# Rotary tables behind the first reciprocal, and finer first transfers, in a one-core encoder block with a product-key expert layer

## The chip, the cores and the metric

The kernel runs on one core of one Trainium2 chip. The metric is the device time of one execution in microseconds (us). TensorE is called PE here, VectorE DVE, ScalarE ACT, GpSimd POOL, and SyncE, which only issues transfers, SP.

## The reference

One layer over 256 tokens of width 1024, batch 1, all in float32:

```python
n = rmsnorm(h, norm_mix)
qa, ka, va, qb, kb, vb, ga, gb = split(n @ w_in)        # 1024 -> 5120 columns
y_a = differential_attention(qa, ka, va, lam, ...)      # 4 heads, partial rotary on q and k
y_b = neighbourhood_attention(qb, kb, vb, na_rpb)       # 8 heads, windows of a grid, bias
merged = sigmoid(ga) * (y_a @ w_proj_a) + sigmoid(gb) * (y_b @ w_proj_b)
h = h + merged @ w_out
h = h + peer_ffn(rmsnorm(h, norm_ffn), w_query, sub_keys, expert_u, expert_v)
out = rmsnorm(h, norm_final)
```

The rotary part turns the first 16 of each head's 64 dimensions: `rot = concat(x1*c - x2*s, x2*c + x1*s)`, with cosine and sine tables over the positions. The expert layer picks 16 of 16,384 single-neuron experts for each of 8 heads and each token; the kernel computes all experts densely for 240 tokens and gathers rows for the other 16.

## The kernel before

**Tiles.** Every weight matrix is cut into tiles of 1024 x 128, and one stream of them (512 KB each) runs through the whole kernel: tile numbers 0 to 7 are q and k of the differential attention (`T_QA`, `T_KA`), 8 to 11 its v (`T_VA`), 12 to 27 the other attention and the first gates, up to the projections, `w_out` and the queries; then come 128 tiles of the experts' input side (u) and 128 of their output side (v). A tile has 8 chunks (`C`) of 128 rows.

**Each tile is split.** A float32 product is made of three products in a shorter format: the weight tile `raw[t]` becomes a high part `whi[t]` (a rounding copy, on ACT, function `hi`, line L639) and a low part `wlo[t]` (raw minus high, on DVE, `low_w`, L902, for the last tiles of the routing also on POOL, L583). PE then does for each chunk high x high, high x low and low x high, 24 matmuls for a tile (`split_product`, L1412). The activations are split in the same way: `xhi` by `gained_hi` on ACT (L651), `xlo` by `gained_low` on DVE (L913). Four slots (`RAW`, `RING`) hold tiles; SP loads the next tile into a slot when the low part of its old one is done.

**The head.** The activations with the gains come as one array, `xcol`, in four transfers of two chunks each: the first two are issued on ACT's queue, the other two on SP's. Tile 0 comes in two halves (`HALF`, four chunks each; L452 and L453) on SP's queue, ahead of everything else there. Its rounding copy is made on DVE, half by half (L936), and its low half behind each (L938). PE first multiplies ones by ones 12 times (`WARM`, L1578), each as two passes, then takes tiles 0 and 1 together (`two_tiles`): high, low and rest products in an order written out by hand, as the parts come in. Tile 1 is copied on ACT in two halves (L681) behind the eight `gained_hi`.

**The order of DVE's work in the first layer** is written out in one loop over k (the tile that PE is at). At each k DVE does `low_front(k + 3)`, the low part of tile k + 3, and then what else is due: at k = 3 `rms(1)`, which makes the inverse root of the mean square of every token (L919 scales, ACT takes the root, L921 is the reciprocal, into `rstd`); at k = 5 `lambda_rest` (three single-column operations, L961 to L963); and the rotary work `rope(half, part)`, placed by `ROPE_AT = {5: (0, 0), 6: (0, 1), 9: (1, 0), 10: (1, 1)}`. The first call also makes the two `tables` (cos x rstd and sin x rstd, L1003 and L1004, in `mfull`). Then come a shuffle (L1006), two products and a sum (L1008, L1010, L1011). `link(x)` makes DVE wait until its own operation x is complete. PE takes tiles 8 and 9 as a pair (their products stand token by token), and 10 and 11 likewise, so it waits there for the low part of the second tile of the pair (`pe.wait_ge(lo_ready, k + 2)`).

**Later.** While PE works through the u tiles, POOL adds the gates of 128 tokens into a table in DRAM, with 128 indirect transfers one after another (L619), in eight rounds that each wait for the landing of the one before. The first v tile needs the first blocks of that table.

Of the kernel before, what the change touches and what calls it, by code (L numbers as in the profile page):

```python
# [27 lines left out]
F32 = mybir.dt.float32  # L28
F32R = mybir.dt.float32r
U32 = mybir.dt.uint32  # L30
ALU = mybir.AluOpType
# [4 lines left out]
T = 256  # L36
# [44 lines left out]
WARM = 12  # L81
# [106 lines left out]
def build(nc, stream, urows, vrows, const, keys, bias, lamv, gfin, h1_dram, x_dram, a_dram, g_dram, out):  # L188
    with ExitStack() as top:
# [3 lines left out]
        def sem(name):  # L193
            return top.enter_context(nc.semaphore(name))
# [118 lines left out]
        def K(name):  # L313
            a, b = CONST[name]
            return cst[:, a:b]
# [19 lines left out]
        head_landed = sem("head_landed")  # L335
# [3 lines left out]
        x_landed = [sem(f"x_landed{q}") for q in range(4)]  # L339
# [107 lines left out]
        def _(sp):  # L447
            def load_x(q):
                at = slice(N_COL + 2 * q * T if q else 0, N_COL + (2 * q + 2) * T)
                sp.dma_start(xcol[:, at], const["xcol"][:, at]).then_inc(x_landed[q], 16)  # L450

            sp.dma_start(raw[0][:, 0:HALF, :], stream[0, :, 0:HALF, :]).then_inc(head_landed, 16)  # L452
            sp.dma_start(raw[0][:, HALF:C, :], stream[0, :, HALF:C, :]).then_inc(raw_landed[0], 16)  # L453
            load_x(2)
            load_x(3)
            for t in range(1, 3):
                sp.dma_start(raw[t][:], stream[t]).then_inc(raw_landed[t], 16)
# [175 lines left out]
        def _(act):  # L633
# [32 lines left out]
            for q in range(2):  # L666
                at = slice(N_COL + 2 * q * T if q else 0, N_COL + (2 * q + 2) * T)
                act.dma_start(xcol[:, at], const["xcol"][:, at]).then_inc(x_landed[q], 16)
            act.preload_act_table(ACT.Sqrt)
            for c in range(C):  # L670
                act.wait_ge(x_landed[c // 2], 16)
                gained_hi(0, c)
# [215 lines left out]
        def _(dve):  # L888
# [8 lines left out]
            def link(ins):  # L897
                dve.wait_ge(dve_order, mark(ins))
# [34 lines left out]
            for half in range(2):  # L933
                dve.wait_ge(raw_landed[0] if half else head_landed, 16)
                part = slice(half * HALF, (half + 1) * HALF)
                dve.tensor_copy(whi[0][:, part], raw[0][:, part]).then_inc(head_hi, 1)  # L936
                dve.wait_ge(head_hi, half + 1)
                dve.tensor_tensor(wlo[0][:, part], raw[0][:, part], whi[0][:, part].bitcast(F32), ALU.subtract).then_inc(lo_ready if half else head_lo, 1)  # L938
            for c in range(C):
                dve.wait_ge(x_landed[c // 2], 16)  # L940
                gained_low(0, c)
# [54 lines left out]
            def rope(half, part):  # L996
# [17 lines left out]
            for k in range(T_PROJ + 1):  # L1014
# [391 lines left out]
        def _(pe):  # L1406
# [122 lines left out]
            def two_tiles():  # L1529
# [3 lines left out]
                def high(t, c):  # L1533
                    return pe.matmul(dst[t], whi[t][:, c, :], xhi[:, c, :], start=c == 0, stop=False)
# [340 lines left out]
```

## Time and profile before

| what | us |
|---|---|
| timed runs, median of 3 (lowest, highest) | 979.31 (978.58, 981.8) |
| profiled execution, its own time | 978.91 |
| its span, first to last instruction | 977.1 |
| PE matmul busy | 962.4 (98%) |
| DVE busy | 754.2 (77%) |
| ACT busy | 558.0 (57%) |
| POOL busy | 355.4 (36%) |
| mean granted clock of PE | 0.998 |

The profiled execution is one execution; 1.8 us of its time lie outside its span. Times inside the span count from its first instruction. A row of the timeline gives start, length, engine, line, operation, and in brackets how long the engine sat idle before it and what released it.

### The profile page before, as it was taken

To read this page: it belongs to the slowest core of one execution; us is meant where nothing else is said; L and a number is where in the kernel's file an instruction comes from. 1 tells how busy PE (TensorE), PEld (TensorE's weight loads), DVE (VectorE), ACT (ScalarE), POOL (GpSimd) and SP (SyncE) were. 2 spreads that over 40 slices of the span, in tenths; PEclk is the share of its full clock that TensorE was granted. 3 is DMA by queue.
4 is the path that set the end of the run, shared out by engine and by line. 5 is a ranking of instruction groups with operands and counts; after the bars stand their busy time and mean duration, and the time that the engine had idled before them with its cause. 6 is when DMAs were issued, how large, how long until landed. Compare 5 with 4: busy or idle time off the path is not lost.

```text
span 977.1 us, 23876 instructions
## 1 busy us (share of the span) xinstructions
PE 962.4 (98%) x8425; PEld 943.0 (97%) x8425; DVE 754.2 (77%) x1602; ACT 558.0 (57%) x996; POOL 355.4 (36%) x201
## 2 busy tenths in 40 slices
PE   9999999999999999999999998999999999999997
PEld 9989899999999999999999998999999999999997
DVE  7988868879779987776877763777777777677765
ACT  6556854666665656666676663455455455454544
POOL 0000000077888788887888885010001000000000
PEclk9999999999999999999999999999999999999999
DMA  8776667756579889999999998899999999888871
GB/s 304 251 232 209 187 205 233 237 174 216 190 242 242 242 250 291 282 257 310 269 277 298 260 303 245 279 324 321 302 304 319 350 290 310 265 302 289 270 245 45
DMA packets 135875, 254.60 MB, mean 261 GB/s; under 512 B 31648, under 2 KB 80672, under 8 KB 135536
## 3 DMA queue, kind: packets, MB, share of 16 engines
q1 hardware_dynamic: 112048, 235.30, 74.2%
q0 software_dynamic: 23168, 17.12, 9.1%
q8 instruction: 54, 0.88, 0.4%
q10 hardware_dynamic: 576, 1.06, 0.3%
q14 instruction: 29, 0.24, 0.1%
HBM read 227.07 MB, written 26.35 MB: 259 GB/s over the span
## 4 chain that ended last, share of the span: by engine, by line
PE 61%; POOL 23%; DMA 6%; issue 5%; DVE 3%; ACT 1%; ACTq 0%; DVEq 0%
POOL g_scratch L619 23%; PE pO L1412 21%; PE pTT L1711 18%; PE pM L1711 17%; DMA g_scratch<-small 5%; DVE wlos L902 1%; PE pSS L1477 1%; PE pSS L1737 1%; PE pSS L1633 1%; DMA xcol<-in_xcol 1%; POOL wlos L583 0%; DMA held<-g_scratch 0%; PE pM L1516 0%; PE pTT L1496 0%; PE pM L1510 0%
## 5 line engine op out<-in xcount | busy, mean ns | idle before, releaser
L639 ACT ACTIVATE whis<-raw 128x1024 fp32r<-128x1024 f32 x326 | 344.6, 1058 | 224.9 <-PE pM L1711 173.1
L1412 PE MATMUL pO<-xhi,whis 128*128 128x240 f32 (+1 forms) x1040 | 288.2, 277 | 0.0
L1412 PE MATMUL pO<-xlo,whis 128*128 128x240 f32 (+1 forms) x1040 | 286.0, 275 | 0.0
L1412 PE MATMUL pO<-xhi,wlos 128*128 128x240 f32 (+1 forms) x1040 | 285.9, 275 | 0.0
L619 POOL DMA_INDIRECT g_scratch<-small x128 | 237.6, 1856 | 47.0 <-issue 36.8
L1316 DVE TENSOR_TENSOR wlos<-raw,whis 128x1024 fp32r<-128x1024 f32 x125 | 153.2, 1225 | 88.2 <-ACT whis L639 72.8
L902 DVE TENSOR_TENSOR wlos<-raw,whis 128x1024 fp32r<-128x1024 f32 x171 | 207.4, 1218 | 17.4 <-ACT whis L639 16.0
L1412 PEld LDWEIGHTS pO<-xhi,whis 128*128 128x128 f32 x1040 | 196.3, 189 | 2.4 <-issue 2.0
L1412 PEld LDWEIGHTS pO<-xhi,wlos 128*128 128x128 f32 x1040 | 196.4, 189 | 0.0
L1412 PEld LDWEIGHTS pO<-xlo,whis 128*128 128x128 f32 x1040 | 196.2, 189 | 0.0
L583 POOL TENSOR_TENSOR wlos<-raw,whis 128x1024 fp32r<-128x1024 f32 x31 | 74.9, 2424 | 215.3 <-ACT whis L639 215.3
L1711 PE MATMUL pTT<-vhi,whis 128*128 128x240 f32 x512 | 141.7, 277 | 5.7 <-DVE vlo L1312 5.6
L1711 PE MATMUL pTT<-vlo,whis 128*128 128x240 f32 x512 | 140.9, 275 | 0.0
L1711 PE MATMUL pTT<-vhi,wlos 128*128 128x240 f32 x512 | 140.5, 274 | 0.0
L1711 PE MATMUL pM<-vhi,wlos 128*128 128x240 f32 x509 | 139.9, 275 | 0.0
L1711 PE MATMUL pM<-vhi,whis 128*128 128x240 f32 x509 | 139.7, 274 | 0.0
L1711 PE MATMUL pM<-vlo,whis 128*128 128x240 f32 x509 | 139.6, 274 | 0.0
L1711 PEld LDWEIGHTS pTT<-vhi,whis 128*128 128x128 f32 x512 | 97.1, 190 | 9.8 <-DVE vlo L1312 6.6
L785 ACT ACTIVATE ast<-pO 128x240 f32<-128x240 f32 x128 | 47.3, 370 | 99.8 <-PE pO L1412 77.5
L1711 PEld LDWEIGHTS pTT<-vhi,wlos 128*128 128x128 f32 x512 | 97.4, 190 | 0.0
L1711 PEld LDWEIGHTS pTT<-vlo,whis 128*128 128x128 f32 x512 | 97.3, 190 | 0.0
L1711 PEld LDWEIGHTS pM<-vhi,whis 128*128 128x128 f32 x509 | 96.8, 190 | 0.0
(284 smaller groups left out, 1859.9 us busy)
## 6 DMA issues: line engine op xcount, KB each, us to landing
raw<-in_stream SPq DMA_DIRECT2D x199, 512.0 KB
raw<-in_vrows SPq DMA_DIRECT2D x128, 512.0 KB
a_scratch<-ast SPq DMA_DIRECT2D x128, 120.0 KB
held<-a_scratch SPq DMA_DIRECT2D x128, 120.0 KB
g_scratch<-ghot SPq DMA_DIRECT2D x32, 256.0 KB, 4.4
held<-x_scratch SPq DMA_DIRECT2D x16, 512.0 KB
held<-g_scratch SPq DMA_DIRECT2D x124, 64.0 KB
biasm<-in_bias SPq DMA_DIRECT2D x8, 256.0 KB, 4.8
```

The source lines that it names most:

```text
L583: pool.tensor_tensor(wlo[s], raw[s][:], whi[s].bitcast(F32), ALU.subtract).then_inc(lo_ready, 1)
L619: pool.indirect_dma_start(g_dram, bass.IndirectOffsetOnAxis(goff[:, n:n + 1], 0), gval[:, h, k:k + 1], None, compute_op=ALU.add).then_inc( ...
L639: act.activation(whi[s], raw[s][:], ACT.Copy).then_inc(hi_ready, 1)
L785: act.activation(ast[i % 2][:, 0:NU], pO[i % 2][:, 0:NU], ACT.Gelu).then_inc(evac_act, 1)
L902: dve.tensor_tensor(wlo[t % RING], raw[t % RING][:], whi[t % RING].bitcast(F32), ALU.subtract).then_inc(lo_ready, 1)
L1316: dve.tensor_tensor(wlo[s], raw[s][:], whi[s].bitcast(F32), ALU.subtract).then_inc(lo_ready, 1)
L1412: last = pe.matmul(dst, st, mv, start=(c == 0 and q == 0), stop=(c == len(terms) - 1 and q == 2))
L1477: last = pe.matmul(pS[m][:, 0:T], qkT[rows, q0 + h, b * P:(b + 1) * P], qkT[rows, k0 + h, :], start=True, stop=True)
L1633: last = pe.matmul(pS[hp % 2][:, b * NK:(b + 1) * NK], qp[:, hp, b * P:(b + 1) * P], keysT[:, hp, :], start=True, stop=True)
L1711: last = pe.matmul((acc[c] if dst is None else dst)[:, 0:NU], st[s][:, c, :], mv[s], start=opening and n == 0, stop=closing and n == 2)
L1737: last = pe.matmul(pSS[part, half, :], shares[:, row_token(m), :], urow[U_BUFS + m % V_BUFS][:, half * 512:(half + 1) * 512], start=r == 0 ...
```

## The change

It has three parts. The two rotary tables are made at k = 3 right behind the first reciprocal, instead of at k = 5 ahead of the shuffle. The activations come in five pieces of 1, 1, 2, 2 and 2 chunks (three on ACT's queue, two on SP's) instead of four of 2. Tile 0 comes in three pieces of 2, 2 and 4 chunks instead of two of 4, with a copy and a low part for each piece on DVE. The 12 warm-up products become 9, and PE's first products follow the pieces.

```diff
-WARM = 12
+WARM = 9
+X_PARTS = ((0, 1), (1, 2), (2, 4), (4, 6), (6, 8))
+HEAD_PARTS = ((0, 2), (2, 4), (4, 8))
...
-            sp.dma_start(raw[0][:, 0:HALF, :], stream[0, :, 0:HALF, :]).then_inc(head_landed, 16)
-            sp.dma_start(raw[0][:, HALF:C, :], stream[0, :, HALF:C, :]).then_inc(raw_landed[0], 16)
-            load_x(2)
+            for n, (a, b) in enumerate(HEAD_PARTS):
+                sp.dma_start(raw[0][:, a:b, :], stream[0, :, a:b, :]).then_inc(head_landed[n], 16)
             load_x(3)
+            load_x(4)
...
-            for q in range(2):
-                at = slice(N_COL + 2 * q * T if q else 0, N_COL + (2 * q + 2) * T)
+            for q in range(3):
+                at = slice(N_COL + X_PARTS[q][0] * T if q else 0, N_COL + X_PARTS[q][1] * T)
                 act.dma_start(xcol[:, at], const["xcol"][:, at]).then_inc(x_landed[q], 16)
             act.preload_act_table(ACT.Sqrt)
...
-            for half in range(2):
-                dve.wait_ge(raw_landed[0] if half else head_landed, 16)
-                part = slice(half * HALF, (half + 1) * HALF)
+            for n, (a, b) in enumerate(HEAD_PARTS):
+                dve.wait_ge(head_landed[n], 16)
+                part = slice(a, b)
                 dve.tensor_copy(whi[0][:, part], raw[0][:, part]).then_inc(head_hi, 1)
-                dve.wait_ge(head_hi, half + 1)
+                dve.wait_ge(head_hi, n + 1)
...
                 if part == 0:
-                    if half == 0:
-                        dve.tensor_tensor(tables[:, 0, :], K("cos"), rstd[:], ALU.mult)
-                        link(dve.tensor_tensor(tables[:, 1, :], K("sin"), rstd[:], ALU.mult))
                     dve.wait_ge(evac_act, (half + 1) * HA)
...
                 if k == 3:
                     rms(1)
+                    dve.tensor_tensor(tables[:, 0, :], K("cos"), rstd[:], ALU.mult)
+                    link(dve.tensor_tensor(tables[:, 1, :], K("sin"), rstd[:], ALU.mult))
...
-                pe.wait_ge(head_hi, 1)
-                for c in range(HALF):
-                    pe.wait_ge(gain_hi, c + 1)
-                    high(0, c)
-                pe.wait_ge(head_lo, 1)
-                for c in range(HALF):
-                    low(0, c)
-                pe.wait_ge(head_hi, 2)
+                for n, (a, b) in enumerate(HEAD_PARTS[:-1]):
+                    pe.wait_ge(head_hi, n + 1)
+                    for c in range(a, b):
+                        pe.wait_ge(gain_hi, c + 1)
+                        high(0, c)
+                for n, (a, b) in enumerate(HEAD_PARTS[:-1]):
+                    pe.wait_ge(head_lo, n + 1)
+                    for c in range(a, b):
+                        low(0, c)
+                pe.wait_ge(head_hi, len(HEAD_PARTS))
```

How the instructions stand on the engines is shown at three places; line numbers of the changed kernel are 8 to 10 higher in these parts. The first place is DVE from the reciprocal (L921, L930 after) to the second low part of the tiles 10 and 11; before:

```order
L921 RECIPROCAL rstd<-rstd 128x256
L902 TENSOR_TENSOR wlos<-raw,whis 128x1024 x2
L961 TENSOR_TENSOR lam<-lam 128x1
L962 TENSOR_SCALAR lam<-lam 128x1
L963 TENSOR_SCALAR lam<-xcol 128x1
L1003 TENSOR_TENSOR mfull<-cst,rstd 128x256
L1004 TENSOR_TENSOR mfull<-cst,rstd 128x256
L1006 STREAM_SHUFFLE oB<-qkT 128x1024
```

The same stretch of DVE after:

```order
L930 RECIPROCAL rstd<-rstd 128x256
L1029 TENSOR_TENSOR mfull<-cst,rstd 128x256
L1030 TENSOR_TENSOR mfull<-cst,rstd 128x256
L911 TENSOR_TENSOR wlos<-raw,whis 128x1024 x2
L970 TENSOR_TENSOR lam<-lam 128x1
L971 TENSOR_SCALAR lam<-lam 128x1
L972 TENSOR_SCALAR lam<-xcol 128x1
L1012 STREAM_SHUFFLE oB<-qkT 128x1024
```

The two products that write `mfull` moved past the low parts of tiles 7 and 8 and the three small operations. The second place is the start of DVE's program, with what each operation waits for; before:

```order
L936 CAST whis<-raw 128x512 [waits head_landed]
L938 TENSOR_TENSOR wlos<-raw,whis 128x512 [waits head_hi]
L936 CAST whis<-raw 128x512 [waits raw_landed0]
L938 TENSOR_TENSOR wlos<-raw,whis 128x512 [waits head_hi]
L913 SCALAR_TENSOR_TENSOR xlo<-xcol,xhi 128x256 [waits gain_hi,x_landed0] x2
```

And after:

```order
L945 CAST whis<-raw 128x256 [waits head_landed0]
L947 TENSOR_TENSOR wlos<-raw,whis 128x256 [waits head_hi]
L945 CAST whis<-raw 128x256 [waits head_landed1]
L947 TENSOR_TENSOR wlos<-raw,whis 128x256 [waits head_hi]
L945 CAST whis<-raw 128x512 [waits raw_landed0]
L947 TENSOR_TENSOR wlos<-raw,whis 128x512 [waits head_hi]
L922 SCALAR_TENSOR_TENSOR xlo<-xcol,xhi 128x256 [waits gain_hi,x_landed0]
```

There are two more instructions, and the first pair handles half of what it did. The third place is the start of ACT's program, whose first rows issue transfers of `xcol`; before:

```order
L668 DMA xcol<-in_xcol 128x529
L668 DMA xcol<-in_xcol 128x512
L669 ACT_TABLE_LOAD
L651 ACTIVATE xhi<-xcol 128x256 [waits x_landed0] x2
L651 ACTIVATE xhi<-xcol 128x256 [waits x_landed1] x2
```

And after:

```order
L677 DMA xcol<-in_xcol 128x273
L677 DMA xcol<-in_xcol 128x256
L677 DMA xcol<-in_xcol 128x512
L678 ACT_TABLE_LOAD
L660 ACTIVATE xhi<-xcol 128x256 [waits x_landed0]
L660 ACTIVATE xhi<-xcol 128x256 [waits x_landed1]
L660 ACTIVATE xhi<-xcol 128x256 [waits x_landed2] x2
```

The third chunk waits for the second transfer of ACT's queue before, and for the third after; the bytes ahead of it on that queue are the same.

## Rows read from the trace of the kernel before

**Rows 1.** The page: busy time and share of the span of each engine.
```profile
PE 962.4 (98%) x8425; PEld 943.0 (97%) x8425; DVE 754.2 (77%) x1602; ACT 558.0 (57%) x996; POOL 355.4 (36%) x201
```

**Rows 2.** Waits of PE's matmuls: line, released by, us in total, times, longest.
```profile
PE pTT L1711 <- DVE vlo L1312: 5.6, 2, 5.3
PE pO L1412 <- DVE wlos L902: 1.2, 2, 0.8
```

**Rows 3.** The chain that ended last, pieces: start, us, what.
```profile
597.06 6.31 DMA g_scratch<-small
...
612.36 1.64 PE pTT L1711 x6
```

**Rows 4.** Stretches: busy us of PE, PEld, DVE, ACT, POOL (instructions), clock, DMA share, GB/s.
```profile
10.00:20.00 10.00, 10.00 (x85) 9.95 (x85) 9.86 (x14) 7.26 (x11) 0.00 (x0) 1.00 0.86 301
...
30.40:31.30 0.90, 0.15 (x2) 0.00 (x0) 0.90 (x3) 0.71 (x2) 0.00 (x0) 1.00 1.00 398
36.90:37.40 0.50, 0.14 (x2) 0.00 (x0) 0.50 (x3) 0.26 (x1) 0.00 (x0) 1.00 0.42 66
```

**Rows 5.** Timeline of DVE, 22 to 38 us, parts.
```profile
22.03 1.76 DVE L921 RECIPROCAL rstd<-rstd 128x256 f32<-128x256 f32 x1 [0.48 <-ACT rstd L655]
24.84 2.46 DVE L902 TENSOR_TENSOR wlos<-raw,whis 128x1024 fp32r<-128x1024 f32 x2 [1.05 <-ACT whis L639]
...
27.78 0.42 DVE L1003 TENSOR_TENSOR mfull<-cst,rstd 128x256 f32<-128x256 f32 x1
...
28.58 1.35 DVE L1006 STREAM_SHUFFLE oB<-qkT 128x1024 f32<-128x1024 f32 x1
29.97 1.23 DVE L902 TENSOR_TENSOR wlos<-raw,whis 128x1024 fp32r<-128x1024 f32 x1
...
34.95 2.36 DVE L902 TENSOR_TENSOR wlos<-raw,whis 128x1024 fp32r<-128x1024 f32 x2
```

**Rows 6.** Timeline of ACT, 23 to 33 us, parts.
```profile
23.69 1.05 ACT L639 ACTIVATE whis<-raw 128x1024 fp32r<-128x1024 f32 x1
...
27.82 1.05 ACT L639 ACTIVATE whis<-raw 128x1024 fp32r<-128x1024 f32 x1
...
30.87 2.00 ACT L639 ACTIVATE whis<-raw 128x1024 fp32r<-128x1024 f32 x2
```

**Rows 7.** Timeline of POOL where its indirect transfers begin.
```profile
284.42 7.13 POOL L583 TENSOR_TENSOR wlos<-raw,whis 128x1024 fp32r<-128x1024 f32 x3 [3.32 <-ACT whis L639]
291.71 1.74 POOL L619 DMA_INDIRECT g_scratch<-small  x1 [0.16 <-issue]
```

**Rows 8.** Transfers issued in the first 8 us: KB each, median us to landing.
```profile
raw<-in_stream SPq DMA_DIRECT2D x2, 256.0 KB, 3.9
```

**Rows 9.** Timeline of all engines, first 13 us, parts.
```profile
4.71 0.43 DVE L936 CAST whis<-raw 128x512 fp32r<-128x512 f32 x1 [4.71 <-DMA raw<-in_stream]
...
6.25 2.51 ACT L651 ACTIVATE xhi<-xcol 128x256 fp32r<-128x256 f32 x6 [0.43 <-DMA xcol<-in_xcol]
...
6.80 0.79 PE L1534 MATMUL pO<-xhi,whis 128*128 128x256 f32 x2 [0.56 <-ACT xhi L651]
...
6.98 3.25 DVE L913 SCALAR_TENSOR_TENSOR xlo<-xcol,xhi 128x256 fp32r<-128x256 f32 x8
...
8.86 1.15 ACT L681 ACTIVATE whis<-raw 128x512 fp32r<-128x512 f32 x2
...
10.15 2.35 DVE L902 TENSOR_TENSOR wlos<-raw,whis 128x1024 fp32r<-128x1024 f32 x2
```

**Rows 10.** Stretches of the warm-up products (tile pM) alone, columns as Rows 4 without POOL.
```profile
1.50:3.00 1.50, 1.50 (x9) 1.50 (x9) 0.00 (x0) 0.00 (x0) 1.00 0.61 162
...
4.70:5.40 0.70, 0.70 (x8) 0.69 (x7) 0.00 (x0) 0.00 (x0) 1.00 1.03 392
```

**Rows 11.** Stretches around the first v tile, columns as Rows 4.
```profile
612.00:615.50 3.50, 3.15 (x15) 3.15 (x16) 3.50 (x7) 0.72 (x2) 0.00 (x0) 0.51 0.81 235
615.50:618.50 3.00, 3.00 (x28) 3.00 (x28) 1.19 (x4) 1.35 (x2) 0.00 (x0) 1.00 0.91 268
```

More of the change, by code:

```diff
@@ L80, with x_part @@
 ROTATED = [(d + HALF_ROT) % (2 * HALF_ROT) if d < 2 * HALF_ROT else d for d in range(32)]
-WARM = 12
+WARM = 9
+X_PARTS = ((0, 1), (1, 2), (2, 4), (4, 6), (6, 8))
+HEAD_PARTS = ((0, 2), (2, 4), (4, 8))
+def x_part(c):
+    return next(q for q, (a, b) in enumerate(X_PARTS) if a <= c < b)
 N_COL = 2 * C + 1
@@ L334, in build @@
         raw_landed = [sem(f"raw_landed{s}") for s in range(RAW)]
-        head_landed = sem("head_landed")
+        head_landed = [sem(f"head_landed{n}") for n in range(len(HEAD_PARTS) - 1)] + [raw_landed[0]]
         second_hi = sem("second_hi")
@@ L338, in build @@
         head_lo = sem("head_lo")
-        x_landed = [sem(f"x_landed{q}") for q in range(4)]
+        x_landed = [sem(f"x_landed{q}") for q in range(len(X_PARTS))]
         const_landed = sem("const_landed")
@@ L448, in load_x @@
             def load_x(q):
-                at = slice(N_COL + 2 * q * T if q else 0, N_COL + (2 * q + 2) * T)
+                at = slice(N_COL + X_PARTS[q][0] * T, N_COL + X_PARTS[q][1] * T)
                 sp.dma_start(xcol[:, at], const["xcol"][:, at]).then_inc(x_landed[q], 16)
-            sp.dma_start(raw[0][:, 0:HALF, :], stream[0, :, 0:HALF, :]).then_inc(head_landed, 16)
-            sp.dma_start(raw[0][:, HALF:C, :], stream[0, :, HALF:C, :]).then_inc(raw_landed[0], 16)
-            load_x(2)
+            for n, (a, b) in enumerate(HEAD_PARTS):
+                sp.dma_start(raw[0][:, a:b, :], stream[0, :, a:b, :]).then_inc(head_landed[n], 16)
             load_x(3)
+            load_x(4)
             for t in range(1, 3):
@@ L664, in tanh_gate @@
                 act.activation(gates[:, j, :], gates[:, j, :], ACT.Tanh, scale=0.5).then_inc(gated, 1)
-            for q in range(2):
-                at = slice(N_COL + 2 * q * T if q else 0, N_COL + (2 * q + 2) * T)
+            for q in range(3):
+                at = slice(N_COL + X_PARTS[q][0] * T if q else 0, N_COL + X_PARTS[q][1] * T)
                 act.dma_start(xcol[:, at], const["xcol"][:, at]).then_inc(x_landed[q], 16)
@@ L670, in _ @@
             for c in range(C):
-                act.wait_ge(x_landed[c // 2], 16)
+                act.wait_ge(x_landed[x_part(c)], 16)
                 gained_hi(0, c)
@@ L931, in normed_low @@
                 dve.tensor_tensor(xlo[:, c, :], gates[:, c, :], xhi[:, c, :].bitcast(F32), ALU.subtract).then_inc(norm_lo, 1)
-            for half in range(2):
-                dve.wait_ge(raw_landed[0] if half else head_landed, 16)
-                part = slice(half * HALF, (half + 1) * HALF)
+            for n, (a, b) in enumerate(HEAD_PARTS):
+                dve.wait_ge(head_landed[n], 16)
+                part = slice(a, b)
                 dve.tensor_copy(whi[0][:, part], raw[0][:, part]).then_inc(head_hi, 1)
-                dve.wait_ge(head_hi, half + 1)
-                dve.tensor_tensor(wlo[0][:, part], raw[0][:, part], whi[0][:, part].bitcast(F32), ALU.subtract).then_inc(lo_ready if half else head_lo, 1)
+                dve.wait_ge(head_hi, n + 1)
+                dve.tensor_tensor(wlo[0][:, part], raw[0][:, part], whi[0][:, part].bitcast(F32), ALU.subtract).then_inc(lo_ready if b == C else head_lo, 1)
             for c in range(C):
-                dve.wait_ge(x_landed[c // 2], 16)
+                dve.wait_ge(x_landed[x_part(c)], 16)
                 gained_low(0, c)
```

## Prediction

> **What bounds the kernel now.** I read the page first: PE's matmuls are busy for 962.4 of 977.1 us [rows 1]. Only what PE waits for, or what delays the one long stretch that PE does not set itself, can change the time. Then PE's waits [rows 2]. One of 5.3 us stands before the first v tile; the other named ones are two waits for a low part made on DVE, 1.2 us together. The change touches only the first 38 us, so its worth is first what PE idles there, and then whether that reaches the end.
>
> The first 38 us hold three places where PE stands still. The first is in the head: the third chunk's high part comes late, because ACT starts `gained_hi` for it only at 6.25, when its transfer has landed, and PE idles 0.56 us until 6.80 [rows 9]. The second and third are at about 30.9 and 37.2: in the stretch 30.40 to 31.30 PE is busy 0.15 of 0.90 us, in 36.90 to 37.40 it is busy 0.14 of 0.50, and DVE is busy for all of both [rows 4]. They are the waits for DVE. The first ends when the low part of tile 9, begun at 29.97, is done at 31.20; the second when those of tiles 10 and 11, begun at 34.95, are done at 37.31 [rows 5]. Between them DVE has only work of its own in a row (rotary products and sum). So DVE's order of work sets when PE starts tiles 8 and 10, and what PE gains or loses before 30 us counts only where DVE moves as well.
>
> **The tables.** They are two products of 256 columns: the first starts at 27.78 and the shuffle behind both at 28.58 [rows 5], so together they hold the shuffle up by 0.80 us. Nothing is added or removed, they are moved. Their new place is behind the reciprocal, which ends at 22.03 + 1.76 = 23.79. The next row of DVE starts at 24.84, after 1.05 us of idling for ACT's copy of tile 7 [rows 5], which itself runs from 23.69 to 24.74 [rows 6] and depends on nothing that moves. Two products with their wait (0.80) end at about 24.6 and leave 0.25 us of that hole. They cost nothing there; without the hole they would delay tiles 7 and 8 by 0.80 and win nothing. Behind the hole all is as before until the shuffle, which starts at 27.78. The low part of tile 9 then starts at 29.17 and ends at 30.40; ACT's copy of that tile is done at 27.82 + 1.05 = 28.87 [rows 6], so nothing new is late. PE starts tile 8 0.80 us sooner, and the wait of some 0.8 us is just used up. The low parts of tiles 10 and 11 start at 34.15 instead of 34.95; ACT has both copies at 32.87 [rows 6]. The wait at 37.2 stays as long as it was, 0.80 us sooner. Saved: 0.80 us at 37 us, as far as the trace shows. Bounds: 0.80 (the full length of the two) above; below 0.55, if the link behind the tables and the changed order cost 0.25.
>
> **The finer pieces.** Three chains must be priced. (a) DVE's. Two copies and two low parts of four chunks take 6.98 - 4.71 = 2.27 us, 1.135 a pair [rows 9]. A pair of two chunks costs at least half, 0.57, and at most the whole. A 256-column operation of DVE takes 0.42 (the table product, [rows 5]) or 3.25 / 8 = 0.41 (`xlo`, [rows 9]); the copy of 512 columns 0.43, so one of 256 lies between 0.22 and 0.43. I take 0.42 + 0.30 and 0.04 between them, 0.76 a small pair. The chain becomes 2 x 0.76 + 1.135 = 2.65, 0.38 longer. Against it stands an earlier start. The first transfers land 3.9 us after their issue [rows 8]. At the rate then reached, 392 GB/s [rows 10], the 256 KB of weights and the 264.5 KB of activations, which share the engines, take 1.3 us; half of them 0.65. So the first piece lands about 0.65 sooner, at 4.05, and DVE comes to `xlo` at 6.70 instead of 6.98. If it does not land sooner at all, at 7.36. (b) ACT's. The bytes ahead of the third chunk on its queue are the same, so it lands just before 6.25 as now, give or take 0.1 for one more transfer on each queue; the six copies until 8.76 and those of tile 1, which end at 8.86 + 1.15 = 10.01 [rows 9], stay. DVE takes tile 1 at 10.15 [rows 9]: it can come at most 0.1 sooner, since then it waits for ACT. (c) PE's. Between 5.6 and 6.8 it gets chunks 0 and 1 sooner but not chunk 2, and from 6.80 its queue is as before: the same idle time, longer and earlier. From 10 to 20 us PE and DVE are both busy without a break (10.00 and 9.86 of 10 us [rows 4]), so DVE's shift at 10.15 is carried on. The head is worth +0.1 at best, -0.38 at worst. I take 0, since (a) is a gain that ACT caps.
>
> The trace has the first transfer's data phase only by its rate. In the Trainium skill, "DMA: Bandwidth & Descriptors", section "Anatomy of one DMA", a transfer costs some 2 us fixed and only the rest by bytes at 436 GB/s; that is for POOL's queue. By its figure, 128 KB fewer land 0.3 us sooner, and DVE would come to `xlo` at 4.4 + 2.65 = 7.05, 0.07 later than now instead of 0.28 sooner. No row here shows a piece of this size.
>
> **To the end.** Behind 38 us PE is without long waits until the first v tile, and DVE, ACT and SP wait on its tiles, so all come 0.80 sooner. The v tiles wait for POOL's chain: its last indirect transfer starts at 597.06, and PE starts at 612.36 [rows 3]. That chain begins at 291.71, right behind POOL's last low parts, which start when ACT's copy releases them after 3.32 us of idling [rows 7]. ACT goes by PE's tiles, so the chain starts 0.80 sooner too and, if it takes as long, ends so.
>
> **The sum.** 978.91 - 0.80 + 0 = 978.1 for the profiled execution. The median of the timed runs, 979.31, lies 0.4 above it, so 978.5 on that scale; I say 978.3. One timed run stands at 981.8, so a median of a few runs can differ by more than the gain. The bound of 0.3%, about what a measurement of this kernel can tell from no change, is 2.9 us.
>
> **Rivals.**
> *The gain is given back.* Either (a) comes out long (0.38), or POOL's chain of 128 indirect transfers, which shares the transfer engines with the weights, takes 0.8 longer; since PE idles 5.3 us before the first v tile anyway, its end decides, not PE. Speaks for it: rounds that wait on landings of 6.31 us [rows 3]. Against: nothing in it changes. Time 978.9 to 979.4.
> *Slower: the clock rises late.* The warm-up products run at 9 in 1.5 us until 3.0 but at 8 in 0.7 from 4.7 on [rows 10]: PE went from half to full pace between, though the column reads 1.00 for both. With 9 products, 18 passes, they end at about 4.7 instead of 5.4, and PE then has two products until 6.8. Should the clock be low when tile 0 comes, the price is that of 612.0 to 615.5: 15 products in 3.5 us at 0.51, against 28 in 3.0 at 1.00 [rows 11], so 3.5 us at half pace lose 1.9 us. Of this 0.6 is free, the idle time before tile 10; a time above before needs over 0.6 + 0.8 = 1.4 us lost, half pace from 6.8 until after 9.6. Time then 979.5 to 980.5. Against: the products still fill PE until 4.7, by when it had its full pace [rows 10]. This is the rule that speaks against the change; in the Trainium skill, "TensorE: Matmul & The Clock Gate", Part 1, low is the default state and activity lifts it; the trace agrees, as it drops to 0.51 behind the 5.3 us wait [rows 2, 11].
> *More than forecast.* If POOL's chain ends sooner by chance of its transfers and the wait before the first v tile shrinks enough for the clock to stay up, 1.9 us come on top [rows 11]: 976 to 977.5. Nothing in the change aims there.
> *The move does nothing.* If ACT's copy of tile 7 came early, the hole would be gone. ACT makes it behind the root for the same reciprocal, whose end DVE waits for [rows 5], so both shift together; I leave this at little, inside the first rival.
>
> **How the numbers follow.** Forecast (977.6 to 978.8) 0.52; given back 0.24; slower by the clock 0.09; more than forecast 0.10; anything larger, such as another phase of transfers along POOL's chain, 0.05. The range takes in the forecast, the first rival, the near half of the other two and the scatter of the timed runs: 976.9 to 980.1. Faster by over 0.3% would need under 976.4 and has 0.07, from the third rival and the rest; slower by over 0.3%, over 982.2, 0.05; the same 0.88.
>
> **What would show it.** In the changed profile: the two products that write `mfull` at about 23.8, DVE idle some 0.25 us before the low part of tile 7, which stays at 24.8; the shuffle at 27.8; no wait of PE near 30.5, and the wait near 36.4 still there. In the head, the first copy on DVE near 4.05, `xlo` near 6.7, the low part of tile 1 near 10.1, chunk 2 on PE at 6.8. POOL's first indirect transfer near 290.9, the first v tile near 611.6. I am wrong if the third chunk's transfer lands 0.3 or more off, if PE's first products run at half pace, or if POOL's chain changes its length by more than a microsecond.

## The result

| kernel | median, us (20 executions each) | lowest to highest |
|---|---|---|
| before | 979.53 | 975.38 to 981.84 |
| changed | 982.98 | 977.0 to 985.22 |

The ratio is 1.0029, 95% interval 1.0016 to 1.0042: the change costs 2.8 us by the ratio (0.0029 x 979.5), 3.45 by the medians. It is just inside the bound of 0.3%, but on the other side of where I put it, and the median lies outside the range. The profiled execution of the changed kernel took 983.00 us, its span 981.2, against 977.1 before; the mean granted clock is 0.994 for 0.998.

PE's waits in the changed kernel (line, released by, us in total, times, longest):

```profile
PE pTT L1721 <- DVE vlo L1320: 5.2, 2, 4.9
PE pO L1542 <- ACT xhi L660: 3.1, 1, 3.1
PE pM L1588 <- POOL ones L586: 1.0, 1, 1.0
PE pO L1701 <- DVE wlos L911: 0.8, 1, 0.8
...
PE pO L1420 <- DVE wlos L911: 0.2, 1, 0.2
```

The wait for DVE's low parts, 1.2 us in two pieces before [rows 2], is down to 0.2. A new one of 3.1 us stands in the head, for ACT's `xhi`. The timelines of ACT, DVE and PE of that stretch show why; ACT first:

```profile
3.98 0.51 ACT L660 ACTIVATE xhi<-xcol 128x256 fp32r<-128x256 f32 x1 [0.53 <-DMA xcol<-in_xcol]
4.75 0.51 ACT L660 ACTIVATE xhi<-xcol 128x256 fp32r<-128x256 f32 x1 [0.26 <-DMA xcol<-in_xcol]
8.30 2.52 ACT L660 ACTIVATE xhi<-xcol 128x256 fp32r<-128x256 f32 x6 [3.04 <-DMA xcol<-in_xcol]
```

DVE, the same stretch:

```profile
3.81 0.29 DVE L945 CAST whis<-raw 128x256 fp32r<-128x256 f32 x1 [3.81 <-DMA raw<-in_stream]
...
4.56 0.29 DVE L945 CAST whis<-raw 128x256 fp32r<-128x256 f32 x1
...
8.11 0.43 DVE L945 CAST whis<-raw 128x512 fp32r<-128x512 f32 x1 [2.80 <-DMA raw<-in_stream]
```

The first two pieces land sooner than anything before: the first copy starts at 3.81 for 4.71 [rows 9]. The third piece of each queue is 2 us late: chunk 2 starts at 8.30 for 6.25 [rows 9], though the bytes ahead of it on its queue are the same, and the last piece of tile 0 is copied at 8.11. The transfers, issued in the first 8 us (KB each, median us to landing):

```profile
xcol<-in_xcol SPq DMA_DIRECT2D x2, 256.0 KB, 6.7
...
raw<-in_stream SPq DMA_DIRECT2D x2, 128.0 KB, 3.2
...
xcol<-in_xcol ACTq DMA_DIRECT2D x1, 256.0 KB, 6.6
xcol<-in_xcol ACTq DMA_DIRECT2D x1, 136.5 KB, 3.2
xcol<-in_xcol ACTq DMA_DIRECT2D x1, 128.0 KB, 3.5
```

PE in the head of the changed kernel:

```profile
1.01 4.21 PE L1588 MATMUL pM<-ones 128*128 128x128 f32 x18 [1.01 <-POOL ones L586]
4.87 1.03 PE L1542 MATMUL pO<-xhi,whis 128*128 128x256 f32 x2
8.96 0.77 PE L1542 MATMUL pO<-xhi,whis 128*128 128x256 f32 x2 [3.06 <-ACT xhi L660]
```

And the stretches from there and around the first v tile (busy of PE, PEld, DVE, ACT, POOL, then clock, DMA share, GB/s):

```profile
6.50:9.00 2.50, 0.04 (x1) 0.07 (x1) 0.85 (x2) 0.70 (x2) 0.00 (x0) 1.00 1.04 373
9.50:12.80 3.30, 3.30 (x17) 3.30 (x17) 3.30 (x9) 3.18 (x7) 0.00 (x0) 0.50 1.05 403
13.00:16.00 3.00, 3.00 (x28) 3.00 (x27) 2.84 (x3) 1.56 (x4) 0.00 (x0) 1.00 0.72 254
613.60:620.40 6.80, 4.63 (x21) 4.63 (x22) 5.96 (x13) 2.31 (x5) 0.00 (x0) 0.50 0.64 186
620.50:623.50 3.00, 3.00 (x29) 3.00 (x29) 1.39 (x2) 1.35 (x2) 0.00 (x0) 1.00 1.00 347
```

From 9.5 to 12.8 PE runs at a granted clock of 0.50, that is 1.2 for 2.4 GHz: 17 products in 3.3 us, against 28 in 3.0 behind it. Before the clock fell PE had idled 3.06 us. The lost pace comes on top of the late landing, since tiles 0 and 1 go through here. DVE's reciprocal starts 3.44 us later than before (25.47 for 22.03 [rows 5]). Then the tables give back what was forecast:

```profile
25.47 1.75 DVE L930 RECIPROCAL rstd<-rstd 128x256 f32<-128x256 f32 x1 [0.49 <-ACT rstd L664]
27.26 0.42 DVE L1029 TENSOR_TENSOR mfull<-cst,rstd 128x256 f32<-128x256 f32 x1
27.60 0.42 DVE L1030 TENSOR_TENSOR mfull<-cst,rstd 128x256 f32<-128x256 f32 x1
28.28 2.45 DVE L911 TENSOR_TENSOR wlos<-raw,whis 128x1024 fp32r<-128x1024 f32 x2 [0.26 <-ACT whis L648]
...
31.22 1.36 DVE L1012 STREAM_SHUFFLE oB<-qkT 128x1024 f32<-128x1024 f32 x1
```

The tables fill the hole and leave 0.26 us of it; the shuffle is 2.64 us late, 0.80 less than the reciprocal. POOL's chain starts at 294.20 for 291.71 [rows 7], 2.5 us late. The chain of waits then reads:

```profile
600.08 6.12 DMA g_scratch<-small
...
608.19 5.29 DMA held<-g_scratch
...
615.77 1.64 PE pTT L1721 x6
```

The last indirect transfer starts 3.0 us late, the first v tile 3.4 (615.77 for 612.36 [rows 3]), and the end 4.1. The last 0.7 are put down to the clock, which is at 0.50 for 6.8 us there instead of the 3.5 of before [rows 11]. So of 4.1 us in these two executions, 2.5 are there before POOL's chain begins. That part can be followed back to the change; the rest arises in stretches that the change doesn't touch.

### The profile page after: what moved, and what is told of

Same layout as the page of the kernel before. It is cut to its first block, busy times and chain, and to the rows that moved or that the text cites. A ratio compares the mean times of both kernels' runs of the same rounds, so it can differ in the third digit from the quotient of the medians.

```text
span 981.2 us, 23869 instructions
## 1 busy us (share of the span) xinstructions
PE 964.7 (98%) x8419; PEld 945.0 (96%) x8419; DVE 756.5 (77%) x1604; ACT 559.5 (57%) x996; POOL 352.8 (36%) x201
## 4 chain that ended last, share of the span: by engine, by line
PE 62%; POOL 24%; DMA 6%; issue 5%; DVE 2%; ACT 1%; ACTq 0%; DVEq 0%
POOL g_scratch L628 23%; PE pO L1420 21%; PE pTT L1721 18%; PE pM L1721 17%; DMA g_scratch<-small 5%; PE pSS L1485 1%; PE pSS L1747 1%; DVE wlos L911 1%; PE pSS L1643 1%; DMA xcol<-in_xcol 1%; DMA held<-g_scratch 1%; POOL wlos L592 0%; PE pM L1524 0%; PE pTT L1504 0%; PE pM L1518 0%
```

## The experiments

Theory T: the third transfers land late and move everything. Theory C: fewer warm-up products, and idle time behind them, leave PE at half pace in the head. The rival to both is that the tables' move did the harm. Each ratio is to the kernel before on the same chip, with its 95% interval; one unit in the third decimal is about 1 us. Half pace means that PE's products take as long as at 1.2 GHz, full pace as at 2.4 GHz.

**The tables alone.** On two chips:

```diff
 # before: only this, and the two products out of `rope`
...
                 if k == 3:
                     rms(1)
+                    dve.tensor_tensor(tables[:, 0, :], K("cos"), rstd[:], ALU.mult)
+                    link(dve.tensor_tensor(tables[:, 1, :], K("sin"), rstd[:], ALU.mult))
```

> The kernel before with only the two table products moved behind the reciprocal. Theory T (transfers: the third pieces land 2 us late) and theory C (clock: PE idles in the head and then runs tile 0 at half pace) both leave this edit alone: 0.8 us faster than before, ratio about 0.999, the shuffle at 27.8. If the move itself were the harm, it would be 1 us or more slower.

> The move of the tables alone once more, on another chip: the profiled saving at the shuffle was 0.80 us (28.58 to 27.76), but the ratio 0.9974 would be 2.5 us. By the chain of waits alone 0.8 us, ratio 0.999; if the tables' move does more than that, 0.997 to 0.998 again.

Measured: 978.15 us, ratio 0.9974 (0.9961 to 0.9987), and again 978.95, 0.9995 (0.9978 to 1.0012). The rival falls: the tables do no harm. DVE in the first of these profiles:

```profile
23.80 0.42 DVE L1020 TENSOR_TENSOR mfull<-cst,rstd 128x256 f32<-128x256 f32 x1
24.14 0.42 DVE L1021 TENSOR_TENSOR mfull<-cst,rstd 128x256 f32<-128x256 f32 x1
24.82 2.46 DVE L902 TENSOR_TENSOR wlos<-raw,whis 128x1024 fp32r<-128x1024 f32 x2 [0.26 <-ACT whis L639]
...
27.76 1.35 DVE L1003 STREAM_SHUFFLE oB<-qkT 128x1024 f32<-128x1024 f32 x1
```

The shuffle moved from 28.58 [rows 5] to 27.76, 0.82 us; tables at 23.80, idle 0.26, as forecast. POOL's chain starts at 290.89 in this profile and at 291.28 in the other, for 291.71. Whether the time gains 0.8 us or the 2.5 of the first ratio stays open; the two intervals overlap from 0.9978 to 0.9987, which is 1.3 to 2.2 us. The gain can be followed to the start of POOL's chain only: in the first of these profiles that chain takes 307.45 us for the 305.35 of before, and the first v tile comes at 613.64, which is later than before.

**The pieces alone.** The changed kernel with the tables at their old place:

```diff
 # changed kernel; the two products at k = 3 are taken out
...
                 if part == 0:
+                    if half == 0:
+                        dve.tensor_tensor(tables[:, 0, :], K("cos"), rstd[:], ALU.mult)
+                        link(dve.tensor_tensor(tables[:, 1, :], K("sin"), rstd[:], ALU.mult))
```

> The changed kernel with the tables where they were before. Theories T and C: all of the loss is here, 3.5 to 4.5 us slower than before (ratio 1.0035 to 1.0045), the 0.8 us of the tables missing. If the loss came from the tables: no slower than before.

Measured: 983.36 us, ratio 1.0039 (1.0025 to 1.0053). All of the loss is here. Chunk 2 starts at 7.83, and PE runs 10 products in the 1.8 us from 10.10 at a clock of 0.50. Late landing and half pace both come with the pieces and the 9 products; this run does not part them.

**Warm-up products.** One number changed, in the kernel before (twice) and in the changed kernel (12 and 20 products):

```diff
 # before
-WARM = 12
+WARM = 9
 # changed kernel
-WARM = 9
+WARM = 12        # the other: 20
```

> The kernel before with 9 warm-up products for 12, transfers untouched. Theory C alone: PE stands idle longer in the head and some executions see half pace there, 1 to 2 us slower (ratio 1.001 to 1.002). Theory T alone: within 0.3 us of before, the third chunk at 6.8 as before.

> The kernel before with 9 warm-up products once more, since its first interval just reached 1 (0.9997 to 1.0035). Theory C: ratio 1.001 to 1.0025 again, with executions in two groups some 4 us apart. Without theory C: within 0.0005 of 1.

> The changed kernel with 12 warm-up products. Theory C alone: the loss is gone, 0.5 to 1 us faster than before (ratio 0.999 to 1.0). Theory T alone: the third pieces still land at about 8.2 and the loss stays, 2 to 3.4 us slower than before (ratio 1.002 to 1.0035), at most the part of the half pace back.

> The changed kernel with 20 warm-up products, which fill PE until 6.5 to 8 and so most of the wait for the third piece. With theory C on top of T: the clock no longer falls at 9.4 and the time is 1 us or more below that with 12 products, ratio to before 0.999 to 1.0005. With theory T alone: as with 12 products, ratio 1.0005 to 1.0015.

Measured: 9 products in the kernel before, 982.33 us, 1.0016 (0.9997 to 1.0035), and again 981.06, 1.0014 (0.9994 to 1.0033). Neither interval excludes 1 alone; both lie where theory C put them, and their mean, 1.0015, has an interval from about 1.0001 to 1.0029 if the two are taken as independent. The two groups of executions 4 us apart, which I expected of the second, are not plain in its twelve times. The profile shows the half pace directly, stretches of the first of the two:

```profile
7.00:9.90 2.90, 2.90 (x13) 2.79 (x14) 2.90 (x8) 2.90 (x7) 0.00 (x0) 1.00 1.02 412
10.10:11.90 1.80, 1.80 (x10) 1.80 (x10) 1.80 (x4) 1.06 (x1) 0.00 (x0) 1.00 0.97 316
```

The second of these stretches in the kernel before, with 12 products:

```profile
10.10:11.90 1.80, 1.80 (x18) 1.80 (x17) 1.80 (x3) 1.75 (x3) 0.00 (x0) 1.00 0.95 305
```

And in the changed kernel with 20 products:

```profile
10.10:11.90 1.80, 1.80 (x17) 1.80 (x16) 1.58 (x4) 1.80 (x5) 0.00 (x0) 1.00 1.02 405
```

With 9 warm-up products PE does 13 products in 2.9 us and 10 in 1.8, with 12 and with 20 it does 18 and 17 in 1.8: half pace until about 13 us. The clock column reads 1.00 in all of them; so at the head of a program the counts are to be read and not the column. No transfer was touched: chunk 2 starts at 6.35. POOL's chain starts 2.9 us late in this profile (294.64) and 1.3 late in the repeat (293.05), where the pace comes back at about 10 us.

The changed kernel with 12 products: 981.10 us, 1.0009 (0.9994 to 1.0024); with 20, 980.38, 1.0000 (0.9978 to 1.0022). The landings are as late as ever (chunk 2 at 8.28 and 8.58), but PE is not at half pace behind them, and 2 to 3 us are back. PE and DVE with 12 products:

```profile
8.93 0.70 PE L1542 MATMUL pO<-xhi,whis 128*128 128x256 f32 x2 [3.28 <-ACT xhi L660]
```

```profile
12.33 2.35 DVE L911 TENSOR_TENSOR wlos<-raw,whis 128x1024 fp32r<-128x1024 f32 x2
...
15.73 1.23 DVE L911 TENSOR_TENSOR wlos<-raw,whis 128x1024 fp32r<-128x1024 f32 x1
...
24.23 1.75 DVE L930 RECIPROCAL rstd<-rstd 128x256 f32<-128x256 f32 x1 [0.49 <-ACT rstd L664]
```

This parts the two causes. At full pace the late landing alone moves DVE's low part of tile 1 from 10.15 [rows 9] to 12.33 and the reciprocal from 22.03 [rows 5] to 24.23, 2.2 us each; half pace adds the 1.24 us from 24.23 to the 25.47 of the changed kernel. Theory T alone would have left a ratio of 1.002 to 1.0035 for the first run. Its interval reaches into that, so it does not refute this by itself. All four kernels with the late landing and 9 products, however, lie at 1.0029 to 1.0039 with intervals above 1 (two of them follow below), and the two with 12 and 20 at 1.0009 and 1.0000, so theory T is not the only cause. Whether 20 products do better than 12 the intervals leave open.

**More warm-up in the good version.** The tables alone, with `WARM = 16`:

```diff
 # the tables' move alone
-WARM = 12
+WARM = 16
```

> The move of the tables alone, with 16 warm-up products for 12. Theory C (the clock rises late in executions where PE's first stretch of work is too short or broken): the slow executions go, median at or up to 1 us below that of the move alone, ratio to before 0.9965 to 0.9975. Without theory C: 0 to 0.3 us slower than the move alone, since the products end up to 0.5 us after the first chunk is there.

Measured: 980.08 us, 0.9995 (0.9975 to 1.0014). The gain that theory C promised (0.9965 to 0.9975) did not come; the interval also holds a loss of 0.3 us against the move alone. More than 12 bring nothing that shows where the chunks come at 4.9 to 6.3.

**Which transfers.** Each kind of piece alone in the kernel before (12 products, old tables). Only the constants are shown; the transfers, copies and waits follow them:

```diff
 # activations only
+X_PARTS = ((0, 1), (1, 2), (2, 4), (4, 6), (6, 8))
+HEAD_PARTS = ((0, 4), (4, 8))
 # tile 0 only
+X_PARTS = ((0, 2), (2, 4), (4, 6), (6, 8))
+HEAD_PARTS = ((0, 2), (2, 4), (4, 8))
```

> The kernel before with only the activations in five pieces; tile 0 in two halves, 12 warm-up products, tables where they were. If the third piece lands late because of the extra piece on ACT's queue: chunk 2 of xhi at 7.8 to 8.3 instead of 6.25 and 1.5 to 2 us slower (ratio 1.0015 to 1.002). If the pieces of tile 0 are the cause: chunk 2 at 6.2 to 6.4 and no change.

> The kernel before with only tile 0 in three pieces; activations in four, 12 warm-up products, tables where they were. If the pieces on SP's queue make the landings late: chunk 2 or the last piece of tile 0 later than 7, 1 to 2 us slower. If the activations' pieces are the cause: chunk 2 at 6.2 to 6.4, the time of before within 0.5 us.

Measured: activations only 982.06 us, 1.0024 (1.0001 to 1.0047); tile 0 only 979.74, 1.0001 (0.9981 to 1.0022). ACT with the activations in pieces:

```profile
5.22 0.51 ACT L660 ACTIVATE xhi<-xcol 128x256 fp32r<-128x256 f32 x1 [0.53 <-DMA xcol<-in_xcol]
6.67 2.51 ACT L660 ACTIVATE xhi<-xcol 128x256 fp32r<-128x256 f32 x6 [0.95 <-DMA xcol<-in_xcol]
```

And with tile 0 in pieces:

```profile
4.31 1.93 ACT L660 ACTIVATE xhi<-xcol 128x256 fp32r<-128x256 f32 x4 [1.34 <-DMA xcol<-in_xcol]
6.69 1.71 ACT L660 ACTIVATE xhi<-xcol 128x256 fp32r<-128x256 f32 x4 [0.45 <-DMA xcol<-in_xcol]
```

Neither half does what both do: chunk 2 comes at 6.67 in the one and even sooner, at about 5.3, in the other. My expectation for the first (7.8 to 8.3) was wrong as to the landing. Its ratio of 1.0024 lies just above the 1.0015 to 1.002 that I expected with a late landing, without a cause that the profile shows (its one profiled execution took 975.85).

**Count or length of rows.** The first transfer of each queue issued as two of 64 partitions, rows of 2 KB:

```diff
 # before
-            sp.dma_start(raw[0][:, 0:HALF, :], stream[0, :, 0:HALF, :]).then_inc(head_landed, 16)
+            for rows in (slice(0, P // 2), slice(P // 2, P)):
+                sp.dma_start(raw[0][rows, 0:HALF, :], stream[0, rows, 0:HALF, :]).then_inc(head_landed, 16)
...
+                for rows in (slice(0, P // 2), slice(P // 2, P)) if q == 0 else (slice(0, P),):
+                    act.dma_start(xcol[rows, at], const["xcol"][rows, at]).then_inc(x_landed[q], 16)
```

> The kernel before with the first transfer of each queue issued as two of 64 partitions each: as many transfers, with the same bytes, as in the changed kernel, but rows of 2 KB for 1 KB; both are waited for, so no work starts on less. If the number of transfers makes the third one late: chunk 2 of xhi at 7.5 or later, 1.5 to 2 us slower. If the short rows do: chunk 2 at 6.3 to 6.5, within 0.5 us of before.

Measured: 981.26 us, 1.0002 (0.9980 to 1.0025). Chunk 2 is late with long rows too:

```profile
5.88 0.91 ACT L652 ACTIVATE xhi<-xcol 128x256 fp32r<-128x256 f32 x2 [1.68 <-DMA xcol<-in_xcol]
8.03 2.50 ACT L652 ACTIVATE xhi<-xcol 128x256 fp32r<-128x256 f32 x6 [1.24 <-DMA xcol<-in_xcol]
```

But this is not the same delay. The first pieces are late as well here: ACT starts at 5.88 for 4.91, and DVE's first copy at 5.31 for 4.71 [rows 9]. So the run does not show that short rows are not needed; the run with the third piece on SP's queue, below, shows that they are not enough. The expected loss of 1.5 to 2 us is not in the ratio, whose interval reaches to 1.0025.

**What lies behind the third piece.** SP holds the large transfers back until it has landed:

```diff
 # changed kernel
+            sp.wait_ge(x_landed[2], 16)
             for t in range(1, 3):
                 sp.dma_start(raw[t][:], stream[t]).then_inc(raw_landed[t], 16)
```

> The changed kernel, but SP issues the tiles 1 and 2 and all behind them only when the third piece of the activations has landed. If the third pieces are late because the large transfers behind them share the engines: they land at 5.5 to 6.3 instead of 8.2, while tile 1 comes later (about 9.5), so the time is between that of before and that of the change. If they are late by themselves, with three transfers on both queues: still at 7.5 to 8.3, and the time 1 us or more above that of the change.

Measured: 982.33 us, 1.0030 (1.0013 to 1.0048); chunk 2 at 8.02. The large transfers behind are not the cause. SP's two transfers of the activations were not held back. The time is that of the change and not the 1 us above it that I expected. Just before the landing the transfer engines are not even full, at 0.55 of their time and 209 GB/s (columns as in the stretches above):

```profile
6.00:8.00 2.00, 0.00 (x0) 0.00 (x0) 0.18 (x1) 0.00 (x0) 0.00 (x0) 1.00 0.55 209
```

**Spacing and queue.** ACT's third transfer behind the table load, and the same transfer on SP's queue:

```diff
 # later
+                if q == 2:
+                    act.preload_act_table(ACT.Sqrt)
 # on SP's queue
+            load_x(2)
             load_x(3)
...
-            for q in range(3):
+            for q in range(2):
```

> The changed kernel with ACT's third transfer (chunks 2 and 3) issued behind the table load, at about 3.0 instead of 1.7. If the number of transfers issued in the first 2 us makes the third ones late: the last piece of tile 0, third on SP's queue, lands at 6 instead of 8.1, and chunk 2 starts before 8. If three transfers on a queue are late however they are spaced: both stay at 7.5 to 8.5. Time between 0.5 us below and 1 us above that of the change.

> The changed kernel with chunks 2 and 3 of the activations moved from ACT's queue, as its third transfer, to SP's queue, as its fourth, in front of the other two; ACT issues two. If it is three on both queues that makes the landings late: chunk 2 starts at 5.5 to 6.7, tile 0's last piece is there before 6.5, and the time falls to that of before or 1 us below (ratio 0.9985 to 1.0005). If an extra transfer in all does it: chunk 2 at 7.5 or later and no gain against the change.

Measured: the first, 981.35 us, 1.0039 (1.0017 to 1.0061), is no test. ACT issues past a table load, so the transfer left at 1.72 as before and chunk 2 came at 8.00; it counts as the change once more. The second: 982.37 us, 1.0019 (1.0006 to 1.0032). ACT in its profile:

```profile
3.93 0.51 ACT L661 ACTIVATE xhi<-xcol 128x256 fp32r<-128x256 f32 x1 [0.95 <-DMA xcol<-in_xcol]
4.61 0.51 ACT L661 ACTIVATE xhi<-xcol 128x256 fp32r<-128x256 f32 x1 [0.17 <-DMA xcol<-in_xcol]
6.71 2.51 ACT L661 ACTIVATE xhi<-xcol 128x256 fp32r<-128x256 f32 x6 [1.59 <-DMA xcol<-in_xcol]
```

Chunk 2 is back at 6.71 and the last piece of tile 0 is copied at 5.71, with all pieces kept. POOL's chain starts at 291.59, 2.6 us before that of the changed kernel. The time did not follow as I expected. Its profile shows no half pace behind chunk 2; what makes this one execution long is POOL's chain, 309.69 us from the first to the last indirect transfer for 305.35 before. That the 9 products cost the rest in the timed executions is a guess, which the next run tests.

**Both mended.** The same with 12 products:

```diff
 # third piece on SP's queue
-WARM = 9
+WARM = 12
```

> All pieces and the moved tables, the third piece of the activations on SP's queue, and 12 warm-up products instead of 9. The landings were mended by the move to SP's queue, the time was not (ratio 1.0019). If the rest of that loss is the clock, which 9 products leave low in some executions: ratio 0.9985 to 1.0, 1.5 us or more below the 9-product version. If the finer pieces cost in another way: ratio still 1.001 or more.

Measured: 980.44 us, 1.0008 (0.9990 to 1.0026). Lower than with 9 products by 0.0011, less than the 1.5 us expected and within the intervals, so the guess is not shown. Chunk 2 comes at 7.28 here, 1 us later than before, so the move to SP's queue mends the landing only in part. The kernel is not shown to beat the one before.

**A version that beats both?** The tables' move with tile 0 in three pieces and 12 products, on two chips:

```diff
 # before, with the tables moved; transfers, copies and waits follow
+HEAD_PARTS = ((0, 2), (2, 4), (4, 8))
```

> The move of the tables with tile 0 in three pieces, activations in four, 12 warm-up products. If the pieces of tile 0 alone are harmless and only their sum with the activations' is not: the time of the move alone within 0.5 us, ratio to before 0.997 to 0.9995, chunk 2 of xhi no later than 6.4. If an extra transfer on SP's queue costs by itself: 1 us or more above the move alone.

> Moved tables and tile 0 in three pieces, once more on another chip: it had the lowest median of all (977.27) with an interval over 1. If it beats both kernels: ratio 0.997 to 0.9995 with the interval below 1.

Measured: 977.27 us, 0.9991 (0.9971 to 1.0010), and 979.68, 1.0005 (0.9987 to 1.0023). Both ratios are below that of the changed kernel; neither interval is below 1. The only interval of all that is below 1 is that of the first run of the tables' move, and its repeat holds 1.

All profiles side by side, by what the two theories name (times in us; "half pace" is where PE's counts or the clock column show it in the head). The third column is short for where the pieces are: 3 / 3 is three transfers on ACT's queue beside three pieces of tile 0 on SP's:

| kernel | warm-up | transfers of ACT / pieces of tile 0 | chunk 2 starts | half pace behind chunk 2 | first indirect transfer | ratio |
|---|---|---|---|---|---|---|
| before | 12 | 2 / 2 | 6.25 | no | 291.71 | 1 |
| changed | 9 | 3 / 3 | 8.30 | yes | 294.20 | 1.0029 |
| pieces alone | 9 | 3 / 3 | 7.83 | yes | 295.00 | 1.0039 |
| held back | 9 | 3 / 3 | 8.02 | yes | 294.24 | 1.0030 |
| "later" | 9 | 3 / 3 | 8.00 | yes | 294.64 | 1.0039 |
| changed, 12 | 12 | 3 / 3 | 8.28 | no | 293.44 | 1.0009 |
| changed, 20 | 20 | 3 / 3 | 8.58 | no | 293.57 | 1.0000 |
| rows split | 12 | 3 / 3 | 8.03 | yes | 295.55 | 1.0002 |
| before, 9 | 9 | 2 / 2 | 6.35; 6.17 | yes; yes | 294.64; 293.05 | 1.0016; 1.0014 |
| third on SP's queue | 9 | 2 / 3 | 6.71 | no | 291.59 | 1.0019 |
| the same, 12 | 12 | 2 / 3 | 7.28 | no | 291.98 | 1.0008 |
| activations only | 12 | 3 / 2 | 6.67 | no | 291.89 | 1.0024 |
| tile 0 only | 12 | 2 / 3 | 5.34 | no | 291.80 | 1.0001 |
| tables alone | 12 | 2 / 2 | 6.21; 6.28 | no; no | 290.89; 291.28 | 0.9974; 0.9995 |
| tables alone, 16 | 16 | 2 / 2 | 6.35 | no | 291.41 | 0.9995 |
| tables and tile 0 | 12 | 2 / 3 | 5.44; 5.50 | no; no | 291.97; 291.17 | 0.9991; 1.0005 |

With 3 / 3, chunk 2 comes at 7.8 to 8.6 in seven of seven profiles; in every other kernel at 5.3 to 7.3. With 9 products PE is at half pace behind chunk 2 in six of seven, with 12 or more in one of twelve. What decides it is not shown: PE idles 3.28 us ahead of chunk 2 with 12 products and keeps its pace, while with 9 it loses it after 3.06 us, and in the kernel before with 9 it does not have it until 10 to 13 us.

## Why the prediction was wrong

**What bounds the kernel** held as far as the start of POOL's chain: DVE's order decided PE's waits at 31 and 37 us, and shifts there came through (2.64 us at the shuffle, 2.49 at the first indirect transfer in the changed kernel; 0.82 and 0.82 with the tables alone). Beyond that point the chain's own length covers them.

**The tables** held in mechanism and size: two products in a hole of 1.05 us, 0.26 left for the 0.25 forecast, the shuffle 0.82 sooner for 0.80, the wait of 0.8 gone and that of 0.4 kept (the first profile of the tables alone). No working of mine gives the 2.5 us of one ratio.

**The finer pieces, step (b), failed.** I priced the head at 0 because "the bytes ahead of the third chunk on its queue are the same, so it lands just before 6.25 as now". The bytes are the same, but chunk 2 started 2.05 us later. What I left out is that the number of transfers counts beside their bytes, on both queues at once: with either queue at its old count chunk 2 came at 5.3 to 7.3. The term that I put at 0 measured 2.2 us at the reciprocal, at full pace. DVE (a) went as estimated, first piece at 3.81 (estimate 4.05), a small pair 0.75 (4.56 - 3.81) for 0.76, but it then stood 2.80 us for the third piece. By (c) PE idled 3.06 us for the 0.56 of before.

**The clock rival** had the right mechanism and too small a chance and price. I argued that the products "still fill PE until 4.7, by when it had its full pace", from one execution; in the changed one all 18 passes ran at half pace (4.21 us), and PE was at half pace again from 9.5 to 12.8. When the pace rises differs between executions: the 24 passes of 12 products took from 4.40 to 5.49 us. I let 0.6 us of the loss be free in the idle time before tile 10, where [rows 2] leave only 0.4 (1.2 - 0.8). And PE at half pace also holds up ACT, which copies tile 3 only when tile 0 is done, and so DVE, which waits before its low part of tile 3 in the changed kernel and not with 12 products:

```profile
16.84 1.23 DVE L911 TENSOR_TENSOR wlos<-raw,whis 128x1024 fp32r<-128x1024 f32 x1 [1.00 <-ACT whis L648]
```

The slack was thus not there. I also priced the two apart and never together, though both fall on the same stretch. With 12 products the same late landing costs 2.0 us less (1.0009 for 1.0029, intervals that just overlap).

**How large each is.** By POOL's start: tables -0.4 to -0.8; late landing +2.2 to +2.6 (293.44 against the two of the tables alone); clock in the head +0.8 more (294.20), and 1.3 to 2.9 where it stands alone. The sum for the changed kernel is 294.20 - 291.71 = 2.5. In the timed executions, with all runs put side by side: 1.0029 to 1.0039 with late landing and 9 products; 1.0014 to 1.0019 with 9 products and the landing in time; 1.0000 to 1.0009 with late landing and 12 or more; 0.9974 to 1.0024 around a mean of 1.000 with neither. So the loss needs both to reach its full size. The share of the 9 products is 0.0011 to 0.0029 by single pairs, of which hardly one is clear by itself. That of the late landing with 12 or more products (1.0009, 1.0000) is not shown at all, and smaller than the 2.2 us that its profiles show at POOL's start; the intervals reach to 2.4 us, and I can't say where the rest goes.

**To the end.** The chain from POOL's first to its last indirect transfer took 305.35 us before, 305.88 in the changed kernel, and between 298.35 and 309.69 over all nineteen profiles. This term, which I held constant, scatters more than the change is worth. The clock behind the wait at the first v tile adds 1.4 to 3.1 us or not: from the first v tile to the end it takes 363.0 to 363.3 us where the clock stays up and 364.7 to 366.1 where it falls. This is the third rival of the prediction, and it goes some way to explain why executions of one kernel lie 5 to 10 us apart. In the first run of tables and tile 0, the seven executions up to 977.98 us have mean clocks of 0.998 or more, and the five from 979.74 on 0.996 or less. Whether it falls equally often in all kernels is not shown: the clock stayed up in five of the nineteen profiles, none of them with 9 products and none with 3 / 3.

**Left open:** why a few parts of the third transfers stay behind with three on both queues (last section), and whether it is their number or the small size of the pieces ahead of them that counts; what decides whether PE gets and keeps its full pace in the head; how much of the late landing reaches the end; and whether the activations' pieces alone cost anything (1.0024, interval from 1.0001).

## What to carry to other kernels

Splitting first transfers brings the first pieces sooner and may bring the next ones later: give the piece that starts the long run of work its own row in the plan, look at its landing and not at the first one's, and try the split on one queue before both. Do not set the number of warm-up products by one execution or by when the first chunk arrives: three fewer cost some 1.5 us here with no transfer touched (1.0016 and 1.0014), four more brought nothing. An edit placed in a hole that the profile shows (DVE idle 1.05 us) came out to within 0.02 us, while the one priced at nothing by a count of bytes decided the result.

## What was not expected of the hardware

Three transfers on ACT's queue beside three pieces on SP's, about 512 KB on each as before, put off the start of chunk 2 from 6.25 to 7.8 to 8.6 us, in six kernels on several chips (in the run with the first transfers split by rows chunk 2 is late as well, at 8.03, but in another way). The trace also has the times of the sixteen increments by which a landing is counted (`then_inc(..., 16)`), and they say more than the landing alone. For the transfer that chunk 2 waits for, us:

| kernel | eighth | fifteenth | last |
|---|---|---|---|
| before | 5.62 | 5.77 | 6.22 |
| changed | 6.01 | 7.39 | 8.28 |
| changed, 12 | 5.92 | 7.13 | 8.25 |
| changed, 20 | 5.77 | 7.22 | 8.56 |
| pieces alone | 5.97 | 7.59 | 7.80 |
| held back | 6.11 | 7.05 | 7.99 |
| "later" | 5.87 | 6.85 | 7.98 |
| rows split | 7.04 | 7.93 | 8.01 |
| activations only | 6.13 | 6.23 | 6.23 |
| third on SP's queue | 5.75 | 5.93 | 6.68 |
| the same, 12 | 5.83 | 6.89 | 7.25 |

With 3 / 3 half of the increments are there nearly as soon as before, 0.15 to 0.49 us later; one or a few of the sixteen are late by some 2 us, and all work waits for the last one. With the rows split all of them are late, which is why that run is another case. So the wait is not for bytes in sum. In the changed kernel the transfer engines moved 298 GB/s from 3.5 to 6 us, where before they moved 381:

```profile
3.50:6.00 2.50, 2.40 (x11) 1.92 (x9) 1.44 (x4) 1.02 (x2) 0.00 (x0) 1.00 0.88 298
```

That is 0.2 MB less, about 0.5 us at the old rate; what holds the last parts back the runs do not show. ACT's queue issues a transfer past a table load that stands before it in the program (1.72 us, with the load running from 1.69 to 2.97).
